# Gated delta rule with two triangular inversions in flight, masks moved behind the first product, and a re-ordered head preparation

## The reference

```python
q = _l2norm(q) * 128 ** -0.5;  k = _l2norm(k);  beta = sigmoid(beta)
G = cumsum(g) within a chunk;  decay = exp(G_c - G_j) for j <= c, else 0
L = where(strict, beta[..., :, None] * (k @ k.T) * decay, 0.0)
rhs = concatenate([beta[..., None] * v, (beta * exp(G))[..., None] * k], axis=-1)
sol = triangular_solve(eye(64) + L, rhs, lower=True, unit_diagonal=True)
u_t, w = sol[..., :128], sol[..., 128:]
p_intra = (q @ k.T) * decay;  q_dec = q * exp(G);  k_dec = k * exp(g_last - G)

def step(S, inp):                       # over the 8 chunks, S starts as zeros
    U = ut - wt @ S
    o = qt @ S + pt @ U
    S = S * et + kt.T @ U
    return S, o
```

## Time and profile before

| | us |
|---|---|
| time, median of 3 runs | 2673.52 (2666.58 to 2673.84) |
| the profiled execution's own time | 2675.46 |
| its span | 2674.1 |
| delta stage, from the sums for its norms to the last product of `wa2` (1201.9 to 1784.0) | 582.10 |
| PE busy in that stage | 532.12 |
| DVE, ACT, POOL busy in that stage | 312.65, 230.54, 206.76 |

### The profile page before, as it was taken

How to read it: one execution, slowest core, us unless ns; L and a number is a source line. 1 busy time by engine, 2 the same in 40 slices (tenths; PEclk the granted TensorE clock), 3 DMA queues, 4 the chain that set the end, 5 groups by cost and what they waited for, 6 DMA issues and landing times.

```text
span 2674.1 us, 32614 instructions
## 1 busy us (share of the span) xinstructions
PE 2556.8 (96%) x12792; PEld 2095.6 (78%) x12792; DVE 1066.2 (40%) x2249; ACT 977.3 (37%) x1490; POOL 1211.7 (45%) x1597
## 2 busy tenths in 40 slices
PE   7999999999999999998989899999999999999998
PEld 5777888888777888886778788887777887888886
DVE  6974111126854111236655553423345522311112
ACT  4553222234543222244443244424453433322221
POOL 5114655653125656554333233334323654565653
PEclk9999999999999999998999899999998999999998
DMA  4432223225432222232111010122222231223222
GB/s 159 127 105 79 95 85 112 90 92 151 118 95 82 102 92 95 96 112 78 62 48 47 33 48 32 48 96 87 92 75 91 93 117 63 95 93 104 95 87 79
DMA packets 41371, 237.30 MB, mean 89 GB/s; under 512 B 4737, under 2 KB 5889, under 8 KB 18561
## 3 DMA queue, kind: packets, MB, share of 16 engines
q1 hardware_dynamic: 38912, 218.43, 23.3%
q0 software_dynamic: 2304, 16.78, 3.1%
HBM read 214.22 MB, written 4.19 MB: 82 GB/s over the span
## 4 chain that ended last, share of the span: by engine, by line
PE 83%; DVE 10%; ACT 3%; POOL 2%; issue 1%; DMA 1%; SPq 0%; DVEq 0%; ACTq 0%; POOLq 0%
PE PB L1751 67%; PE PB L1787 3%; PE PB L1753 3%; POOL WL L2781 2%; DVE cc L2408 1%; ACT WH L2002 1%; PE PB L1771 1%; PE PB L1763 1%; PE PB L1957 1%; PE PB L1938 1%; PE PB L1823 1%; PE PB L1945 1%; PE PB L1782 1%; DVE cq L2576 1%; PE PB L1985 1%
## 5 line engine op out<-in xcount | busy, mean ns | idle before, releaser
L2781 POOL TENSOR_TENSOR WL<-WR,WH 128x256 fp32r<-128x256 f32 (+1 forms) x1444 | 1042.2, 758 | 760.8 <-ACT WH L2002 760.8
L1751 PE MATMUL PB<-HH,WH 128*128 128x512 f32 x1992 | 807.5, 405 | 13.1 <-ACT HH L2017 10.2
L1751 PE MATMUL PB<-HL,WH 128*128 128x512 f32 x1992 | 784.3, 394 | 1.2 <-DVE HL L2304 1.2
L1751 PE MATMUL PB<-HH,WL 128*128 128x512 f32 x1992 | 520.5, 397 | 2.5 <-POOL WL L2781 2.5
L1751 PEld LDWEIGHTS PB<-HH,WH 128*128 128x128 f32 x1992 | 379.2, 190 | 105.0 <-issue 15.7
L2002 ACT ACTIVATE WH<-WR 128x2048 fp32r<-128x2048 f32 (+1 forms) x209 | 371.6, 1778 | 218.5 <-PE PB L1751 211.7
L1751 PEld LDWEIGHTS PB<-HL,WH 128*128 128x128 f32 x1992 | 379.1, 190 | 79.5 <-issue 4.4
L1751 PEld LDWEIGHTS PB<-HH,WL 128*128 128x128 f32 x1992 | 366.5, 189 | 77.7 <-issue 4.4
L1751 PE MATMUL PB<-BL,WH 128*128 128x512 f32 x848 | 333.9, 394 | 0.8 <-DVE BL L2313 0.8
L1751 PE MATMUL PB<-BH,WH 128*128 128x512 f32 x784 | 311.4, 397 | 2.7 <-ACT BH L2031 2.7
L1751 PE MATMUL PB<-BH,WL 128*128 128x512 f32 x784 | 197.9, 397 | 4.4 <-POOL WL L2781 4.4
(11 more groups left out here) (343 smaller groups left out, 3054.9 us busy)
## 6 DMA issues: line engine op xcount, KB each, us to landing
WR<-in_w_gu SPq DMA_DIRECT2D x66, 1024.0 KB, 4.8
WR<-in_w_dn SPq DMA_DIRECT2D x48, 704.0 KB, 4.0
WR<-in_w_in SPq DMA_DIRECT2D x22, 1024.0 KB, 4.8
WL<-WR POOLq DMA_DIRECT2D x16, 1024.0 KB, 7.0
WR<-in_qkv SPq DMA_DIRECT2D x12, 1024.0 KB, 4.8
WR<-in_w_out SPq DMA_DIRECT2D x8, 1024.0 KB, 4.8
WR<-in_qk SPq DMA_DIRECT2D x8, 1024.0 KB, 4.8
WR<-in_gb SPq DMA_DIRECT2D x4, 1024.0 KB, 4.9
```

The costliest lines, as they stand in the source:

```text
L1751: ins = pe.matmul(out[:, 0:n], wt[:, k * cols + j * P:k * cols + (j + 1) * P], x[:, k, 0:n], start=first, stop=last)
L2781: ins = g.tensor_tensor(m.WL[u % 2][:, part], m.WR[u % 2][:, part], f32(m.WH[u % 2][:, part]), ALU.subtract)
```

## The change

Five edits, all in the delta stage:

1. **Two lanes of inversions.** `ZZ`, `TT`, `YY` exist twice, the lane `inversions` is split into one for even and one for odd heads. The second set lies where `MM`, the raw gates `R` and a constant row stood.
2. **The mask behind the first product.** `i3` multiplies the whole `UM` with `TT`; DVE masks while it empties the bank into `YY`. ACT's copy, `MM` and POOL's `imask` go. The masks of levels 1 to 5 are stored turned over.
3. **The matrix first.** In `prepare` `p11`, `p12` come directly after `p8`, `prow`, `p2`, `p4`; then the head is `ready` and its inversion may start. `p5`, `p13` to `p15`, `p1`, `colsum` follow.
4. **The root later.** `p4` needs only the inverse of the squared norm, and takes it by a reciprocal. Newton's chain becomes the step `p6`, just ahead of `p6v`.
5. **Scans without a first state.** At chunk 0 `c1` has no product (`UU` is copied from `UT`), `c3` no `QD` product, `c4` is one copy. `SS` is never cleared.

```diff
-    dn += [("MM", [P, S]), ("ZZ", [P, S]), ("TT", [P, S]), ("YY", [P, S])]
+    dn += [("ZZ1", [P, S]), ("ZZ", [P, S]), ("TT", [P, S]), ("YY", [P, S])]
+    m.ZZ = [t["ZZ"], t["ZZ1"]]
+    m.TT = [t["TT"], at("TT1", [P, S], spot["Rplace"])[0]]
+    m.YY = [t["YY"], at("YY1", [P, S], con_off + 4 * C_RST)[0]]
@@ ROUGH, the planner's costs
-    "i3": [("T", 0.9, 0), ("A", 0.7, 0)]
+    "i3": [("T", 0.9, 0), ("V", 0.8, 0)]
@@ def prepare(h)
+            room3, t3 = row("p8", h)
+            room, t = row("prow", h, 0)
+            room2, t2 = row("p11", h)
             step("p2", h, tile=t3, q=junk.i, after=junk.after + kn_done[i])
             yield
+            step("p4", h, tile=t, after=dt_after[0] + hf)
+            step("p12", h, tile=t2, after=hf)
+            ready.add(h)
             yield
...
+            room4, t4 = row("p5", h)
+            room, t = row("p13", h)
+            room2, t2 = row("prow", h, 2)
+            step("p1", h, q=qq.i, after=qq.after)
+            step("p9", h, tile=t3, after=hf, st_after=st_after)
             yield
+            step("p14", h, tile=t, after=st_after)
+            step("p15", h, tile=t2, after=st_after)
+            step("p6", h)
+            step("p6v", h, tile=t4, after=hf)
             yield
...
+            qq.free(pe("colsum", "q", h, tile=t, src=m.SQ[qq.i], tok=at("p1q", h), nb=4, j0=0))
+            step("peq", h, tile=t)
@@ def invert(h)
-                if l < 5:
-                    step("imask", h, l + 1, done=done)
+            yield from until((prepared, h))     # ahead of i7u
@@ def scan(gi)
-            step("c0", gi, after=sfree[0] + sfree[1])
+                if n == 0:
+                    step("c1", gi, n, after=sfree[0])
@@ lanes
-        def inversions():
-            for h in range(8):
-                yield from until((prepared, h))
+        def inversions(i):
+            for h in range(i, 8, 2):
+                yield from until((ready, h))
@@ PE
-            te.wait_ge(*(at("im", h) if l == 1 else at("img", h, l)))
-            four(w["tile"], m.MM, m.TT)
+            te.wait_ge(*at("pum", h))
+            four(w["tile"], m.UM[h % 2], m.TT[h % 2])
+                if n > 0:
                     pe.matmul(..., m.SS[n % 2][:, i, :], m.QD[g][:, i, 64 * n:64 * n + 64], start=True, stop=False)
@@ ACT
-        elif kind == "i3":
-            a.activation(m.YY[:], PB[w["tile"].b][:], ACT.Copy).then_inc(sems["iy"], 1)
@@ DVE
-            dv.link(newton(4, r))
-            dv.link(v.tensor_tensor(norms(h, 2), x, r, ALU.mult))
-            dv.link(v.tensor_tensor(norms(h, 1), r, r, ALU.mult))
+            dv.link(v.reciprocal(norms(h, 1), norms(h, 1)))
+        elif kind == "i3":
+            v.tensor_tensor(v4(m.YY[h % 2][:]), v4(PB[w["tile"].b][:]), level(l), ALU.mult).then_inc(sems["iy"], 1)
+            if n == 0:
+                v.tensor_copy(m.UU[0][rows, :, :], m.UT[gi % 2][rows, :, 0:P]).then_inc(sems["c1u"], 1)
@@ POOL
-        elif kind == "imask":
-            g.tensor_tensor(v4(m.MM[:]), v4(m.UM[h % 2][:]), level(l), ALU.mult).then_inc(sems["img"], 1)
```

More of the change, by code:

```diff
@@ L1142, in prepare @@
             cfree[f"k{i}"] = [t.done, kt_done]
-            yield from fbank.left(1)
-            room, t3 = row("prow", h, 2)
-            yield
-            step("p15", h, tile=t3, after=st_after)
-            room.free(at("pel", h))
-            cfree[f"q{i}"] = [t.done, at("pqd", h), at("p1q", h)]
+            step("p15", h, tile=t2, after=st_after)
+            room2.free(at("pel", h))
+            cfree[f"q{i}"] = [t.done, at("pqd", h), at("p1q", h)]
+            step("p6", h)
+            step("p6v", h, tile=t4, after=hf)
+            room4.free(at("pbv", h))
+            kn_done[i] = [at("pbv", h), at("pdn", h)]
+            yield
+            yield from fbank.left(0)
+            room = fbank.take()
+            t = Tile(room, room.after)
+            qq.free(pe("colsum", "q", h, tile=t, src=m.SQ[qq.i], tok=at("p1q", h), nb=4, j0=0))
+            step("peq", h, tile=t)
+            room.free(at("peq", h))
             yield
-        ifree = {n: f for n in "ZTYM"}
+        ifree = {n + str(i): f for n in "ZTY" for i in range(2)}
         def invert(h):
@@ L1155, in invert @@
             st_after = halves[f"store{g}"]
-            step("i1", h, z_after=ifree["Z"], m_after=ifree["M"])
+            step("i1", h, after=ifree[f"Z{i}"])
             yield
@@ L1206, in scan @@
         def scan(gi):
-            step("c0", gi, after=sfree[0] + sfree[1])
+            if gi == 0:
+                step("c0", after=f)
             for n in range(8):
-                yield from fbank.left(1)
-                room1 = fbank.take()
-                t1 = Tile(room1, room1.after)
-                pe("c1", gi, n, tile=t1, after=sfree[n % 2])
-                room1.free(at("c1u", gi, n))
+                if n == 0:
+                    step("c1", gi, n, after=sfree[0])
+                else:
+                    yield from fbank.left(1)
+                    room1 = fbank.take()
+                    t1 = Tile(room1, room1.after)
+                    pe("c1", gi, n, tile=t1, after=sfree[n % 2])
+                    room1.free(at("c1u", gi, n))
                 yield
@@ L1356, in operands @@
                 yield
-        weave(clock, products(), 0.0, lane(gates(), preparations()), inversions(), scans(), gatings(), last_gating(), operands())
+        weave(clock, products(), 0.0, lane(gates(), preparations()), inversions(0), inversions(1), scans(), gatings(), last_gating(), operands())
     def band_attention(xs):
@@ L1891, in tensor_program @@
             te.wait_ge(*at("pbv", h))
[L1892 removed]
+            four(w["tile"], m.ZZ[h % 2], m.bv[h % 2])
         elif kind == "i7w":
@@ L1896, in tensor_program @@
             te.wait_ge(*at("pbk", h))
-            four(w["tile"], m.bk[h % 2], m.ZZ)
-        elif kind == "c1":
+            four(w["tile"], m.bk[h % 2], m.ZZ[h % 2])
+        elif kind == "c1" and key[1] > 0:
             gi, n = key
```

147 lines of the change are left out of this document (64 added, 83 removed), and 4 rows, old and new, of the table ROUGH.

## The result

The changed kernel takes 2645.76 us (median of 5 runs, 2639.49 to 2654.8) against 2673.84 us (5 runs, 2666.58 to 2678.68). The ratio is 0.9896 with a 95% interval of 0.9868 to 0.9924: 28 us faster. A second comparison on another chip gave 0.9897 (0.9883 to 0.9911). The forecast was 2639 within 2616 to 2662. The profiled execution took 2641.71 us, 4 us under its median, so profile against profile the gain is 33.8 us.

What follows compares the result with a forecast made beforehand. The delta stage's length was taken as PE's work plus PE's waits, with a clock term. Terms -3.4, -6.8, -5.8, -9.8, -8.5 sum to -34.3 us: 2641 for the profiled execution, median 2639 us, range 2616 to 2662 (8 in 10).

Steps and rivals of the forecast that it cites:

- PE's work: Scans' first chunk: the c1 products and two QD products of four scans go, all on the path, -3.4 us.
- The scans' start: PE's four waits at scans' first product, 8.8 us, shrink to 2.0 us for the copy of UT, -6.8 us.
- Norms and transpose: In prepare, PE's waits for q's squares (4.2 us) and silu of cv (1.6 us) go as colsum and p5 move later, -5.8.
- Inside inversions and scans: Six causes' waits of 22.3 us fall with short covers to 7.5, plus 5 charged for DVE: 12.5 stay, -9.8 us.
- root: Newton's 3.6 us chain on DVE moves from before UM to ahead of p6v; claimed worth nothing by itself.
- The charge for DVE: DVE gains about 22 us of work, three full stretches instead of one; +5 us of PE waits charged.
- the waits move: Rival, chance 0.10: engines serving two chains make as many short waits, clock stays; only 12 us go, 2661 us.
- DVE becomes the bound: Rival, chance 0.07: masks queue on DVE behind a convolution or Newton's chain, holding up PE; +14 us, 2687 us.
- the 10 and the 30 that were to decide: Sign: PE's waits for YY and ZZ together below 10 us favour the forecast, over 30 the rival of DVE.
- The port between DVE and POOL: DVE instructions on two SBUF operands slow beside POOL's splits; said to change no sign, no size or chance given.
- The clock: Of 14 us lost to the granted clock outside the stage's first 58 us, 8.5 go along with the waits; bounds 0 and 14.
- Outside the stage: Sign: time outside the delta stage should not move by more than 2 us, nor a WL wait grow behind it.

Runs made afterwards that it cites:

- cleared_state: Changed kernel with the scans' edit undone: SS cleared at each scan's start, first chunk's products with the state back; 2656.9 us, ratio 0.9938.
- one_lane: Changed kernel with all eight inversions in one lane again, one after the other; 2654.0 us, ratio 0.9921.
- old_prepare: Changed kernel with the preparation's order of before, an inversion starting only when its head is wholly prepared; 2651.1 us, ratio 0.9907.
- costs_all: Changed kernel with the planner's costs raised for preparation and inversion steps, plus two safety waits of DVE, so the order moves; 2649.4 us, ratio 0.9908.
- root_first: Changed kernel with Newton's root back in front of the matrix's scale, planner's cost included; 2641.7 us, ratio 0.9879.
- costs_start: Changed kernel with the planner's costs raised for the preparation's chain (p4, p6) only, so only the order moves; 2650.5 us, ratio 0.9914.
- the first set of experiments: First four experiments, beside the kernel before: the changed kernel again (2647.0 us) and three kernels undoing the second lane, the preparation's order or the root's place.
- short_splits: Changed kernel, same order, POOL making only the last 256 of 2048 columns of the delta stage's low weight halves (result incomplete); 2624.6 us, ratio 0.9814.
- dma_splits: Changed kernel with the root on ACT and the delta stage's low weight halves made by ACT's negated copy and an adding DMA; 2630.5 us, ratio 0.9844.

## Why the prediction was right, and where it wasn't

**PE's work, -3.4.** 16 products (32 records) are gone from the stage's count. Their price alone wasn't measured: in `cleared_state` they and the waits come to 11 us.

**The scans' start, -6.8.** 8.8 became 1.3 us, 2.0 was forecast. Shown by undoing it (10.7 us of `SS`). Right. Together with the products it is worth 11 us of time x clock in the changed kernel and 7 in the one before, half or a third of the 21 that the change gives.

**Norms and transpose, -5.8.** 5.8 became 1.3 (`RHLr` 0.9 and `SQ` 0.4, neither at the old place). Right.

**Inside inversions and scans, -9.8.** For the waits that this term spoke of, the number is right: 10.0 us are left (`TT` 6.0, `YY` 4.0), forecast 12.5. How far waits go with short covers the runs tell better than the prediction's count did, which took four dense products as the limit (50 pairs, then 17). By the count of pairs under 1.9 us there were 70 before, 68 in one_lane, 46 in old_prepare and 37 in the changed kernel, with 22.3, 19.3, 14.0 and 10.0 us inside levels: some 0.3 us a pair. costs_all breaks the rule, with 17 pairs and still 11.6 us (`YY` 8.8, `TT` 1.7, `ZZ` 1.1). The step that failed is the one on the **root**: "nothing by itself, as no inversion's start is on PE's path unless PE waits". The root's place is in fact worth nothing. But the sentence took the starts' cover from the order of before, where it was 22 to 57 us, and the count of covers ran over the 120 pairs inside inversions and left out the eight starts. With the matrix first and the inversion allowed at `ready`, it is 8.6 to 13.2 us, `ZZ` is ready 8.9 to 15.0 us after the decay row, and six of eight starts wait: 10.9 us that stood in no term. Hence 35.2 us of idle time instead of 25 to 30.

**The charge for DVE, +5.** DVE's busy time rose by 21.8 us, as forecast (22). The price of a full queue was set too small. Taking work out of DVE's way cut the idle time by 5.5 us (the root alone), 10 (the masks, with their order) and 17 (POOL's splits shortened), whereas five other orders of the same work (one_lane, old_prepare, root_first, costs_start, costs_all) left it at 35 to 40. At least 4.0 us of that price stood in the kernel before as well, so it is no measure of what the edit added. So the rival *the waits move*, at 0.10, describes what a better order would do from here, and the rival *DVE becomes the bound* names the right engine with the wrong size: its two waits, `YY` and `ZZ`, came to 14.9 us, between the 10 and the 30 that were to decide.

**The port between DVE and POOL.** "Changes no sign" held, but it was treated as a detail and is worth 17 us of idle time in the changed kernel. 4.0 of them, the `STAT` wait at the stage's head, stood in the kernel before in the same place. How much of the rest did wasn't measured.

**The clock, -8.5.** From the windows, (1 - 0.96) x 582.1 = 23.3 us were lost before and (1 - 0.97) x 552.2 = 16.6 after, 6.7 less. Over the runs of the first set of experiments, the time lost (a run's time times one less its clock) was 54.2 us on the mean for before and 47.6 for the changed kernel. The size is right, as far as a clock rounded to 0.01 over a stage tells (each of the two figures is good to 3 us). But some 2 us of it fell in the first 58.1 us, where the granted clock rose from 0.85 to 0.89 and which the term had left out. That it goes with the waits isn't shown: `short_splits`, with the fewest waits, has 0.985, and `dma_splits`, with 30.5 us of idle time, 0.987.

**Outside the stage.** It gained 0.8 us before it and 3.0 after it, where 2 were allowed; behind the stage PE's busy time fell from 855.9 to 850.6 us for the same products, which is the clock. The two profiles of one kernel differ by as much, so nothing hangs on it. The prediction had also named a wait for `WL` that grows behind a faster stage: behind the stage PE waits 3.2 us for it, before 1.7.

**The sum.** That the profiles' gain, 33.8, met the sum of 34.3 is luck. Idle time gave 14.8 us where the terms had 22.4. PE's busy time in the stage fell by 15.1 us, 11.7 more than the products' 3.4; the products left being the same, that is put down to the clock of this one execution. The medians say 28. In time x clock, which leaves the clock out, the change gives 21 us where the terms without the clock add up to 25.8.

## What to carry to other kernels

When an edit lets a chain start earlier, count the cover ahead of its start as well, not only between its steps: "the start isn't on the path" is a statement about the old order. And when several orders of the same work leave PE idle for the same time, stop moving work and take some out of the queue that all of them wait for. Here 13 instructions of 128 x 4 elements a head were worth more (7 us of time x clock) than any other order tried, and the engine whose splits cost the most (POOL) was one for which PE hardly waited.

## What the runs showed of the hardware

DVE's smallest instructions suffer most from POOL, in proportion to their length: 0.16 us alone, 0.65 to 0.72 beside a split. One line of Newton's chain in the stage of the changed kernel (shortest/median/longest ns):

```profile
L2281 DVE SCALAR_TENSOR_TENSOR NEWT<-NEWT x51: 161/163/722, 1205.7 to 1717.3; 128x4 f32<-128x4 f32 x48, 128x8 f32<-128x8 f32 x3
```

A median of 163 ns says nothing of this; the longest does. With POOL's splits shortened, DVE's busy time in the stage fell by 26.5 us for the same 722 instructions. A table load on ACT costs 1.28 us each time; the Trainium skill ("ScalarE activation tables: per-element evaluation and per-set limits", What a function is on this engine) gives 1283 ns for a change between two functions of different sets, and the eight rows at line 2147 have exactly that. And the granted clock moves a stage of 570 us by 5 us between two executions of one kernel with nearly the same waits, so a change of a few microseconds is to be read from waits and from time x clock, not from one profile's length.
